# Two orders changed in the attention stage of a one-core decoder step: the sample transposes behind the prompt's value matmuls, and the split of the queries one item later

## The reference

```
s = einsum('bqhd,bkhd->bhqk', q, k) * HEAD_DIM ** -0.5
s = s + (cq[..., :, None] - ck[..., None, :])          # cumulated forget values
s = where(k_pos <= q_pos, s, min)
p = softmax(s, axis=-1)
o = einsum('bhqk,bkhd->bqhd', p, v)
out = (o * silu(z)) @ w_out
```

## Time and profile before

| | us |
|---|---|
| three runs | 2480.89, 2475.14, 2481.35 |
| median | 2480.89 |
| profiled execution, own time | 2480.89 |
| profiled execution, span | 2479.0 |
| PE busy | 2227.3 (90%) |
| DVE busy | 1314.7 (53%) |
| POOL busy | 1072.3 (43%) |
| ACT busy | 951.9 (38%) |

### The profile page before, as it was taken

The page is one execution under the profiler, slowest core; times in us unless marked ns, Lnnn a source line. Parts: engine busy times, 40 slices in busy tenths (PEclk is TensorE's granted clock), DMA queues, the critical chain, the costliest instruction groups (busy, mean ns, idle before and its releaser), DMA issues.

```text
span 2479.0 us, 47140 instructions
## 1 busy us (share of the span) xinstructions
PE 2227.3 (90%) x16540; PEld 1916.8 (77%) x16540; DVE 1314.7 (53%) x1892; ACT 951.9 (38%) x1617; POOL 1072.3 (43%) x715
## 2 busy tenths in 40 slices
PE   5999999999349998979999999979888888988999
PEld 3999999999138998969999787745555555558998
DVE  4689888988791016565776211124544544434332
ACT  4556556655451013222222122324444444443121
POOL 0698899889673213443334333222222222211231
PEclk7999999999789999989999999989998999988999
DMA  3222222222133121132322778999999999963112
GB/s 112 65 70 75 80 67 69 74 75 71 37 122 122 46 77 59 64 133 98 123 80 94 265 263 324 346 349 398 388 381 375 389 368 356 388 252 107 52 59 83
DMA packets 137488, 430.97 MB, mean 174 GB/s; under 512 B 23889, under 2 KB 40658, under 8 KB 136162
## 3 DMA queue, kind: packets, MB, share of 16 engines
q1 hardware_dynamic: 121554, 375.94, 41.4%
q0 software_dynamic: 13168, 41.58, 4.7%
q10 hardware_dynamic: 2592, 11.14, 1.1%
HBM read 386.81 MB, written 43.87 MB: 174 GB/s over the span
## 4 chain that ended last, share of the span: by engine, by line
PE 57%; POOL 15%; DVE 11%; issue 8%; ACT 6%; DMA 2%; ACTq 0%; SPq 0%; POOLq 0%; DVEq 0%
POOL ACC L1346 7%; PE PS L602 6%; PE PS L600 6%; PE PS L601 6%; PE PS L698 5%; PE PS L700 5%; PE PS L699 5%; PE PS L765 4%; PE PS L821 4%; PE PS L874 3%; PE PS L901 3%; PE PS L889 2%; POOL ML L1376 2%; PE PS L608 2%; POOL WL L1319 2%
## 5 line engine op out<-in xcount | busy, mean ns | idle before, releaser
L1319 POOL TENSOR_TENSOR WL<-RAW,WH 128x1024 fp32r<-128x1024 f32 (+1 forms) x121 | 306.2, 2531 | 603.7 <-ACT WH L954 598.6
L1658 DVE SCALAR_TENSOR_TENSOR PS<-UX,CWT,PS 128x1024 f32<-128x1024 f32 (+1 forms) x672 | 466.3, 784 | 0.0
L633 PE MATMUL PS<-HH,WH 128*128 128x384 f32 (+1 forms) x1152 | 378.5, 329 | 20.7 <-DVE HL L1644 20.7
L635 PE MATMUL PS<-HH,WL 128*128 128x384 f32 (+1 forms) x1152 | 377.4, 328 | 0.0
L634 PE MATMUL PS<-HL,WH 128*128 128x384 f32 (+1 forms) x1152 | 377.2, 327 | 0.0
L1346 POOL TENSOR_TENSOR ACC<-ACC,PROD 128x1088 f32<-128x1088 f32 x112 | 284.9, 2544 | 31.4 <-ACT PROD L1006 25.2
L698 PE MATMUL PS<-GH,WH 128*128 128x384 f32 (+1 forms) x792 | 271.0, 342 | 25.5 <-DVE KC L1770 12.1
L700 PE MATMUL PS<-GH,WL 128*128 128x384 f32 (+1 forms) x792 | 262.8, 332 | 0.0
L699 PE MATMUL PS<-GL,WH 128*128 128x384 f32 (+1 forms) x792 | 261.7, 330 | 0.0
L633 PEld LDWEIGHTS PS<-HH,WH 128*128 128x128 f32 x1152 | 217.3, 189 | 24.7 <-issue 13.7
L954 ACT ACTIVATE WH<-RAW 128x1024 fp32r<-128x1024 f32 (+1 forms) x121 | 131.4, 1087 | 253.4 <-PE PS L602 218.0
(11 more groups left out here) (213 smaller groups left out, 4348.2 us busy)
## 6 DMA issues: line engine op xcount, KB each, us to landing
KV<-ck SPq DMA_DIRECT2D x256, 512.0 KB, 7.7
KV<-cv SPq DMA_DIRECT2D x256, 512.0 KB, 7.2
RAW<-wA SPq DMA_DIRECT2D x48, 512.0 KB, 3.3
RAW<-wP SPq DMA_DIRECT2D x16, 640.0 KB, 3.9
zT_scr<-ZS ACTq DMA_DIRECT2D x16, 544.0 KB, 2.7
Z<-zT_scr SPq DMA_DIRECT2D x16, 544.0 KB, 3.6
RAW<-wB SPq DMA_DIRECT2D x17, 512.0 KB, 3.3
RAW<-wO SPq DMA_DIRECT2D x16, 512.0 KB, 3.3
```

The lines of the kernel that those rows point to most:

```text
L633: pe.matmul(out, WH[w][:, kk], HH[:, k, a:b], start=k == 0, stop=False)
L635: mm = pe.matmul(out, WL[w][:, kk], HH[:, k, a:b], start=False, stop=k == KD - 1)
L1319: pool.tensor_tensor(WL[s][:, 0:n], RAW[s][:, 0:n], WH[s][:, 0:n].bitcast(F32), ALU.subtract).then_inc(s_lo, 1)
L1658: i = dve.scalar_tensor_tensor(out=o, in0=x, scalar=w[:, j:j + 1], in1=o, op0=ALU.mult, op1=ALU.add)
```

## The change

On PE, inside a slot, the call of `decode_side` is moved behind the calls of `prompt_pv`. Odd slots have no `prompt_pv`, so they stay as they are. In 32 even slots there is both a `decode_side` with work in it and a `prompt_pv`: 24 with side transposes (L808), 3 with L800, 3 with L791 and 2 with the new scores.

On POOL, `split_queries` is called for the item `x // 2 + 1` and not for `x // 2 + 2`, and its own wait for the scores is gone. `load_queries` stays at `x // 2 + 3`.

```diff
@@ PE, loop over the slots
                 if late is not None:
                     i = late
                     decode_tick(late)
-                if late is not None:
-                    decode_side(late, evacs(x - 1))
                 if t == 0 and b > 0:
                     prompt_pv(b - 1, NQ - 1)
                 if t >= 2 and t % 2 == 0:
                     prompt_pv(b, t // 2 - 1)
+                if late is not None:
+                    decode_side(late, evacs(x - 1))
@@ POOL, before the loop and in it
             split_queries(0)
-            split_queries(1)
             load_v(0)
...
                 if t % 2 == 0:
-                    if x // 2 + 2 < NQ * PAIRS:
-                        atleast(pool, s_s, x - 2)
-                        split_queries(x // 2 + 2)
+                    if x // 2 + 1 < NQ * PAIRS:
+                        split_queries(x // 2 + 1)
                     if x // 2 + 3 < NQ * PAIRS:
                         atleast(pool, s_s, x)
                         load_queries(x // 2 + 3)
```

## The result

The changed kernel takes 2492.4 us, the median of 8 runs (2489.28 to 2494.33), against 2481.0 for the kernel before (8 runs, 2471.35 to 2485.32). The ratio is 1.0052, 95% interval 1.0035 to 1.0069: slower by 8.7 to 17 us. The forecast was 2491. The profiled execution took 2492.78 us. Two launches that took far longer than all others (6159 us of the kernel before, 4376 us of the last experiment) are in no ratio of this document.

The account below looks back on a forecast made before the run. It took PE's list, with short round trips to ACT and DVE, to bound the attention stage. Terms 7.7 - 2.7 + 1.0 + 4.6 + 0 = +10.6 us on 2480.89 gave 2491 us, range 2474 to 2502.

Parts of the forecast that it names:

- side transposes, 10 small items: Slots with items of one to four blocks: PE's L821 waits for the copy, 0.65 us each, +6.5 us.
- five and six blocks, 5 items: Side-transpose slots: PE loses 0.65 us, but the next copy wait is up to 0.3 to 0.5 earlier; +1.2 us.
- seven and eight blocks: Six side-transpose slots (t = 6 or 2) where PE waits for ACT anyway: 0.
- no early tick behind: Side-transpose slots whose next slot has no early tick: transposes and a scores item cover the copy: 0.
- L800, three slots: Transpose of the new rows: value matmuls fill PE's wait for sample exponentials; -2.7 us, bounds -6.3 and 0.
- last five slots: New scores and transpose of the result: DVE waits for the moved side work; +1.0 us, range 0 to 6.5.
- pair starts: PE waits for POOL's later query split at pairs 1, 3, 4 and 5, after four DMAs: +4.6 us.
- key splits and scaling: POOL's key split meets DVE's scaling in six pairs: 6 us, against about 5 today; 0, ends -4 and +6.
- Waits that swallow it: Rival: ACT and DVE waits swallow most of the PE loss; about +4, 2485 us; chance 0.31 with POOL off the path.
- The sooner product: Rival: gated product and next maximum come sooner, 0.59 us won in most of 21 slots; 2470 us; chance 0.14.
- POOL off the path: Rival: POOL's order is off PE's path everywhere, leaving +6.0, 2487 us; chance 0.31 together with waits that swallow most.
- Key splits on top: Rival: POOL's key splits meet DVE in all six pairs, costing +6 more: 2497 us; chance 0.08.

Follow-up runs that it names:

- the last experiment: Kernel before with queries split one item later, a pair's first split ahead of POOL's wait, key split at slot 11: 2472.57 us, 0.9979.
- small items: Kernel before with only side transposes moved behind the value matmuls, in slots with items of 1 to 4 blocks: 2482.12 us, 1.0022.
- moving them away: Changed kernel with the key split at slot 11 of a pair, not slot 9: 2485.77 us, 1.003 against the kernel before.
- large items: Kernel before with only side transposes moved behind the value matmuls, in slots with items of 5 to 8 blocks: 2476.72 us, 0.9983.
- the first-split experiment: Changed kernel with a pair's first query split ahead of POOL's wait for the gated product: 2484.7 us, 1.0038 against the kernel before.
- the POOL part alone: Kernel before with only the queries split one item later, PE's order as before: 2491.54 us, 1.0049.
- the PE part: Kernel before with only the side work moved behind the value matmuls, POOL as before: 2482.57 us, 1.0016.
- the L800-only kernel: Kernel before with only the transpose of the new rows moved behind the value matmuls, three slots: 2469.44 us, 0.9958.
- the PE part without the five slots: Kernel before with only side transposes (L808) and new rows (L800) moved behind the value matmuls, POOL as before: 2482.1 us, 1.0024.

## Why the prediction was right, and where a size was off

The time (2491 against 2492.4) and the mechanism hold: no waits swallow it, PE's list is longer by its own short waits. One term, the key splits, was 4 us too small, and that the time was met so closely all the same is in part luck. The terms of the sum:

| term | predicted us | measured |
|---|---|---|
| side transposes, 10 small items | 6.5 | steps 0.73 to 0.77 each, 7.5 for ten; alone +5.5 |
| five and six blocks, 5 items | 1.2 | 1.22 at the four clean ones, 0.4 at the fifth (slot 30) between kernels of full clock |
| seven and eight blocks | 0 | 0 |
| no early tick behind: slots 36, 78, 120 | 0 | 0.10, -0.35, -0.14 |
| L800, three slots | -2.7 | steps -1.3, 0, -1.3; alone -10.4 |
| last five slots | 1.0 | steps 0.16, 0, 0.55, 0, 0.28: 1.0; alone +0.5 |
| pair starts | 4.6 | steps 5.0, of full clock 4.7; mending them 3.5 |
| key splits and scaling | 0 | steps: 9.5 less the 5.5 of before, about 4; moving them away 5.5 |
| sum | 10.6 | 11.4 by the medians, 12.9 by the ratio; the steps add to 16 |

**The copy.** Predicted 0.65 in each small item, from 0.60 of ACT and 0.05 of release; it came to 0.69 of wait and 0.75 of step. The argument on the next exponential (ACT, not DVE, is last for up to four blocks) is what the earlier trace rows and slot 56 now show side by side, and the small and large items apart confirm it. The forecast had the exponential of three blocks 0.4 us later; it came 0.22 later. Its border was drawn a block too low: the maximum over five blocks takes 0.82 us, so by the forecast's own formula (0.6 + 0.82 + 0.47 = 1.9 against 2.0) five blocks are still late by 0.1, and the slots of five blocks lost more (0.41 to 0.43) than those of six (0.19).

**The pair starts.** Predicted with release 1.85, 0.54, 1.64 and 0.59 for pairs 1, 3, 4 and 5; the steps against the first-split experiment are 1.80, 0.74, 1.63 and 0.84, and at full clock the second is 0.63. (The 0.07 us for a release is in no row; slot 18 above shows 0.05, from 1737.13 to 1737.18.) For pairs 2 and 6 the forecast was that the moved side transposes hide the late split. That holds: the POOL part alone loses 0.89 at each, the PE part 0.76 and 0.75, and both together 0.76 and 0.75, not the sum.

**The key splits: the term that was mis-sized.** The step said that the meetings of today (about 5 us on PE) and those to come (6 us) cancel. The first half holds, the second does not. In the kernel before the meetings of pairs 1, 2 and 5 fall on the second head of their item, so that PE stands for them at L889 one item later (slots 24, 40 and 88); that of pair 3 falls on the first (slot 54):

```profile
1762.83 0.98 PE L889 MATMUL PS<-FCON,PP 128*128 128x128 f32 x7 [0.56 <-DVE PP L1971]
...
1837.82 1.75 PE L889 MATMUL PS<-FCON,PP 128*128 128x128 f32 x7 [1.08 <-DVE PP L1971]
...
1911.45 0.98 PE L889 MATMUL PS<-FCON,PP 128*128 128x128 f32 x7 [0.79 <-DVE PP L1971]
...
2063.27 0.98 PE L889 MATMUL PS<-FCON,PP 128*128 128x128 f32 x7 [0.85 <-DVE PP L1971]
```

The kernel with L800 moved and the key split later has no wait at these four places. Against it the kernel before is longer by 0.6 us over slots 22 and 24, 2.2 over 38 and 40 (0.75 of the clock against 0.85 at slot 40), 1.8 over 54 and 56, and 0.9 over 86 and 88: 5.5 us. The steps of slots 22, 38 and 86 alone hide this, since the cost stands in the next one. The changed kernel meets the scaling of the first head in six pairs. Less the side work, it is longer than kernels without a meeting by 1.4, 1.3, 1.3, 1.7, 2.2 and 1.5 us: 9.5, where 6 was forecast. So the term is about 4 us and not 0. PE's waits for the scaling at L889 in slots 22, 38, 70, 86 and 102 are 1.84, 2.35, 1.85, 2.69 and 2.00 us, against 0.46, 0.97, 0.25, 1.32 and 0.62 in the kernel with L800 moved and the key split later: 1.4 to 1.6 us more each, about what DVE lost (2.05 to 2.38 less 0.69). The forecast had taken 1.1 to 1.2 us for each. The lower clock in four of these steps comes on top.

The scaling ended 0.49 us after POOL's subtraction here and 0.48 in the earlier trace rows, less than the 0.69 us that it takes alone, so the rule of the page "SBUF — State Buffer", section "Who interferes with whom" (the Trainium skill), that the later one stands for the other's whole instruction, fits the trace nearly. It spoke for a term nearer to the upper end, +6, than to 0, and about 4 lies there.

**What made up for it.** No term of the sum did: by the steps they add to 16 us. Between the two profiles the stretch from the first to the last mask matmul grew by 15.6 us, which fits, but the whole execution by 11.9 only. 3.4 us came back behind the last scores, where nothing was changed. The windows from there to the last value matmuls, first of the kernel before, then of the changed one, hold the same 65 matmuls:

```profile
2238.80:2252.20 13.40, 10.19 (x65) 7.94 (x65) 4.19 (x10) 6.60 (x13) 2.36 (x1) 0.50 0.23 69
```
```profile
2254.00:2264.80 10.80, 6.72 (x65) 5.38 (x65) 4.33 (x12) 6.62 (x13) 2.36 (x1) 0.89 0.20 54
```

At a clock of 0.50 they take 13.4 us, at 0.89 10.8; nine of the fourteen traces, the changed kernel's among them, have 10.8. So the profile of before had a slow stretch there that most do not have, and that nearly offset the 4 us of the key splits: luck. The times of many executions leave more room; 16 lies inside their 8.7 to 17. The PE part measured +4.0 (1.2 to 6.9), where 6.0 was forecast and the steps of its terms show 7.4; the POOL part measured +12.1, where its steps show about 14. The parts alone add to 16.1, of which 0.89 and 0.89 are the shared starts of pairs 2 and 6; the other 14.3 agree with the 12.9 (8.7 to 17) of both together. Why the PE part comes out below its own steps is open.

**The rivals.** Waits that swallow it: out, the waits for L1266 at L808, L901 and L776 shrank by 5.7 us only (15.1 + 3.8 + 3.0 against 8.5 + 7.7), against 14.6 more at L821. The sooner product: out, slot 56. POOL off the path: out, the pair starts. Key splits on top: half true, the cost came, but the time of 2497 did not.

## What to carry to other kernels

Work moved behind other work of the same engine pays or costs by what covers its round trip: an engine-to-engine copy of 0.60 us is free with 1.75 us of matmuls behind it, and worth 0.75 us of the step without them. Look for the wait that has ready work behind it and move only that (L800 here), not everything that looks alike. A meeting of two engines costs only when somebody waits for the loser. That wait can stand one step behind the meeting, so compare both steps with those of a kernel without it, and size the meetings of the new order by where in the item they will fall.

## What the runs showed of the hardware

The granted clock of PE falls to half for stretches in this stage, at different places in each profile, and so blurs a comparison of small pieces. Windows of 14 us, each from about 0.7 us before the first mask matmul of slot 112, in the kernel before, the changed kernel, the L800-only kernel and the one with large items; the third number from the end is the clock:

```profile
2169.00:2183.00 14.00, 11.04 (x75) 7.09 (x67) 3.73 (x14) 5.77 (x20) 2.19 (x6) 0.65 1.02 405
```
```profile
2190.00:2204.00 14.00, 11.35 (x133) 6.92 (x132) 6.88 (x20) 8.86 (x26) 4.80 (x11) 1.00 1.02 406
```
```profile
2170.00:2184.00 14.00, 11.71 (x137) 7.22 (x130) 7.17 (x20) 8.55 (x26) 2.47 (x6) 1.00 1.02 405
```
```profile
2173.00:2187.00 14.00, 11.03 (x109) 7.04 (x102) 5.11 (x16) 6.82 (x20) 1.69 (x5) 0.88 1.02 402
```

The value matmuls of this slot (x20) took 2.40 us at half the clock in the kernel before and 1.31 at the full one in the changed kernel. Over 221 runs of all these kernels, time falls with the mean granted clock of the run, within kernels: about 4.5 us for each 0.01, correlation -0.57. One of these runs, of the kernel before, has a clock of 0.911 at an ordinary time (2480.85 us); all others lie between 0.947 and 0.964, and without it the slope is 7.0 us and the correlation -0.69. This is a correlation: whether the clock sets the time, or longer waits lower the clock, it does not tell. Brought to the same clock with either slope, as an estimate, the PE part without the five slots is still about +7, large items alone 0 to +1, small items +7 to +8 and L800 alone -7: the gap between the pieces and the whole shrinks to some 6 us, does not close, and stays open.

What a meeting costs DVE can be read off these traces closely. Wherever the scaling took longer than alone, the one of 896 columns ended 0.48 to 0.49 us after POOL's instruction and the one of 384 columns 0.21 to 0.23 after it; alone they take 0.69 and 0.42. In both cases the meeting thus costs what is left of POOL's instruction when the scaling starts, less 0.2 us, whatever the length of the scaling: 896 columns came to 2.05 to 2.73 us in the changed kernel, 384 columns to 1.56 to 2.12 with the key split later. It also happens while POOL is still issuing a DMA in front of the split: in the kernel before, at slot 22, POOL issues one from 1760.67 to 1761.23 (L1557) and casts the keys from 1761.23 to 1762.28 (L1550), and the scaling that started at 1761.02 took 1.75 us, to 0.49 us after the cast.
